# The normalised token rows keep their feature order, and the expert gather reads its stationary blocks with a step of eight elements

## The reference, cut to what matters

```
t = rmsnorm(x, norm_ffn)                       # (320, 1024)
combine = two experts of one group per token   # router
act = silu(t @ w_gate[e]) * (t @ w_up[e]) * combine
x = x + sum over e of act @ w_down[e]
```

## Time and profile before

| | |
|---|---|
| runs without the profiler | 1128.38 us median of 3 (1127.12 to 1129.35) |
| the profiled execution | 1124.03 us, its span 1122.3 us |
| PE busy, share of span | 947.8 us, 84% |
| DVE, ACT busy | 645.9 us (58%), 447.1 us (40%) |
| mean granted clock of PE | 0.921 |
| DMA | 203.33 MB, mean 181 GB/s |

### The profile page before, as it was taken

The page is one execution under the profiler, slowest core; times in us unless marked ns, Lnnn a source line. Parts: engine busy times, 40 slices in busy tenths (PEclk is TensorE's granted clock), DMA queues, the critical chain, the costliest instruction groups (busy, mean ns, idle before and its releaser), DMA issues.

```text
span 1122.3 us, 12426 instructions
## 1 busy us (share of the span) xinstructions
PE 947.8 (84%) x4149; PEld 688.6 (61%) x4149; DVE 645.9 (58%) x1206; ACT 447.1 (40%) x665; POOL 39.3 (4%) x75
## 2 busy tenths in 40 slices
PE   5899999999888687765699966989998999899685
PEld 3476776777554445432467755777777777677363
DVE  2329993001335545423647347788877787888574
ACT  0221102213122233122422044767766776677542
POOL 4000004000000000000000010000000000001100
PEclk9899999999859798897899976999999999999988
DMA  8042355332220676676303241877787788688501
GB/s 226 1 150 98 127 185 181 115 114 75 79 72 10 192 240 221 215 236 260 115 29 134 75 149 67 317 284 303 313 309 291 290 322 319 257 318 309 199 1 47
DMA packets 58069, 203.33 MB, mean 181 GB/s; under 512 B 8761, under 2 KB 9081, under 8 KB 51863
## 3 DMA queue, kind: packets, MB, share of 16 engines
q1 hardware_dynamic: 49280, 185.19, 45.5%
q10 hardware_dynamic: 6031, 9.19, 3.1%
q0 software_dynamic: 2704, 8.27, 2.3%
HBM read 188.96 MB, written 14.03 MB: 181 GB/s over the span
## 4 chain that ended last, share of the span: by engine, by line
PE 45%; DVE 9%; SPq 6%; issue 4%; ACT 4%; DMA 0%; DVEq 0%; POOL 0%; ACTq 0%
PE bank L1957 10%; PE bank L1959 10%; PE bank L1958 10%; PE bank L1948 5%; SPq L345 3%; SPq L348 3%; PE bank L2043 2%; PE bank L1879 2%; PE bank L2149 1%; PE bank L1844 1%; PE bank L2067 1%; DVE act_lo L1505 1%; PE bank L1797 1%; DVE h_tok L1360 1%; PE bank L1853 1%
## 5 line engine op out<-in xcount | busy, mean ns | idle before, releaser
L1669 PE MATMUL bank<-scratch,ring 128*128 128x320 f32 x896 | 242.5, 433 | 0.0
L1669 PEld LDWEIGHTS bank<-scratch,ring 128*128 128x128 f32 x896 | 169.8, 190 | 70.6 <-issue 0.5
L1454 DVE TENSOR_TENSOR pieces<-ring,pieces 128x1024 fp32r<-128x1024 f32 x144 | 173.3, 1222 | 43.3 <-ACT pieces L592 40.7
L592 ACT ACTIVATE pieces<-ring 128x1024 fp32r<-128x1024 f32 x144 | 150.8, 1060 | 76.7 <-PE bank L1959 70.2
L592 ACT ACTIVATE proj<-bank 128x512 f32<-128x512 f32 (+4 forms) x73 | 36.3, 506 | 157.5 <-PE bank L1669 117.0
L1081 DVE SCALAR_TENSOR_TENSOR proj<-scratch,par_w,proj 128x256 f32<-128x256 f32 x240 | 73.7, 380 | 1.1
L1957 PE MATMUL bank<-pieces,act_ft 128*128 128x512 f32 x96 | 43.0, 448 | 28.6 <-DVE act_lo L1505 28.6
L1454 DVE TENSOR_TENSOR last_piece<-ring,last_piece 128x1024 fp32r<-128x1024 f32 x48 | 58.6, 1221 | 2.3 <-ACT last_piece L592 0.3
L592 ACT ACTIVATE scratch<-bank 128x512 f32<-128x512 f32 (+5 forms) x42 | 20.5, 520 | 97.1 <-PE bank L1879 42.1
L592 ACT ACTIVATE last_piece<-ring 128x1024 fp32r<-128x1024 f32 x48 | 51.0, 1062 | 13.7 <-PE bank L1959 13.7
L1844 PE MATMUL bank<-ident,ring 128*128 128x128 f32 x256 | 38.3, 315 | 13.6 <-ACT proj L592 6.4
(11 more groups left out here) (384 smaller groups left out, 1665.1 us busy)
## 6 DMA issues: line engine op xcount, KB each, us to landing
ring<-in_w_expert_gate SPq DMA_DIRECT2D x16, 2048.0 KB, 7.9
ring<-in_w_expert_up SPq DMA_DIRECT2D x16, 2048.0 KB, 8.2
ring<-in_w_expert_down SPq DMA_DIRECT2D x16, 2048.0 KB, 7.8
ring<-in_w_in SPq DMA_DIRECT2D x14, 2048.0 KB, 7.8
ring<-in_cache_k SPq DMA_DIRECT2D x64, 256.0 KB, 3.2
ring<-in_cache_v SPq DMA_DIRECT2D x64, 256.0 KB, 3.1
moe_rows<-att ACTq DMA_DIRECT2D x16, 512.0 KB, 4.5
ring<-in_w_branch SPq DMA_DIRECT2D x3, 2048.0 KB, 9.9
```

The lines of the kernel that those rows point to most:

```text
L592: return F(out, in_, ACT.Copy)
L1454: TT(piece_of[r % 4][:, 1, :], raw_piece(EXPERTS + 3 * e, r), piece_of[r % 4][:, 0, :].bitcast(F32), ALU.subtract).then_inc(s("lo_ready"), 1)
L1669: m = MM(bank[t % 4][:, 0:T], slot(j, DC, GROUP)[:, k, (t % 4) * P:(t % 4 + 1) * P], h[:, k, :], start=k == 0, stop=k == DC - 1)
```

## The change

ACT's L838 and DVE's L1360 write `h_tok` in the order in which they read `x1`. The stationary block k is then every eighth element from k on, a step of 32 bytes; the view `h_of` names it, and the gather reads it. No instruction is added, removed or moved on any engine, and the moving operand, the PSUM banks and all waits are as they were. The last two pieces of the diff stand in a branch for crowded experts that these inputs do not take.

```diff
@@ (tiles)
         h_tok = in_place("h_tok", "gates", 0, [P, 5, D])
         PICK_OF = (0, 1, 0, 1, 2)
+        h_of = h_tok[:, :, :].rearrange("p i (m k) -> p i k m", k=DC)
@@ (ACT)
             def h_tok_hi(b):
                 act.wait_ge(s("rstd_ready"), 1 + b // 2)
-                F(by_parts(h_tok[:, (0, 1, 4)[b], :], DC), by_rows(x1[:, b, :], DC), ACT.Identity, scale=rstd[:, b:b + 1]
+                F(h_tok[:, (0, 1, 4)[b], :], x1[:, b, :], ACT.Identity, scale=rstd[:, b:b + 1]
                   ).then_inc(s("h_tok_hi_ready"), 1)
@@ (DVE)
-                STT(by_parts(h_tok[p, lo_, :], DC), by_rows(x1[p, b, :], DC), rstd[p, b:b + 1],
-                    by_parts(h_tok[p, hi_, :].bitcast(F32), DC), ALU.mult, ALU.subtract).then_inc(s("h_tok_ready"), 1)
+                STT(h_tok[p, lo_, :], x1[p, b, :], rstd[p, b:b + 1], h_tok[p, hi_, :].bitcast(F32), ALU.mult, ALU.subtract
+                    ).then_inc(s("h_tok_ready"), 1)
@@ (PE, gather)
                     for c in range(2):
-                        f = slice((2 * j + c) * P, (2 * j + c + 1) * P)
                         for i_ in range(5):
-                            m = MM(b_[:, c * 2 * P:(c + 1) * 2 * P], h_tok[:, i_, f],
+                            m = MM(b_[:, c * 2 * P:(c + 1) * 2 * P], h_of[:, i_, 2 * j + c, :],
                                    pick_t[:, PICK_OF[i_], :, :].rearrange("p u n -> p (u n)"), start=i_ == 0, stop=i_ == 4)
@@ (PE, the branch not taken)
-                        MM(bank[k % 4][:, t0:t0 + P], h_tok[:, i_, f].bitcast(F32), ident[:, :], start=i_ == 0, stop=i_ > 1,
+                        MM(bank[k % 4][:, t0:t0 + P], h_of[:, i_, k, :].bitcast(F32), ident[:, :], start=i_ == 0, stop=i_ > 1,
```

More of the change, by code:

```diff
@@ L2095, in _ @@
                         pe.wait_ge(s("h_hi_ready"), k - 3)
-                    f = slice(k * P, (k + 1) * P)
                     for i_, t0 in enumerate((0, P, 0, P)):
-                        MM(bank[k % 4][:, t0:t0 + P], h_tok[:, i_, f].bitcast(F32), ident[:, :], start=i_ == 0, stop=i_ > 1,
+                        MM(bank[k % 4][:, t0:t0 + P], h_of[:, i_, k, :].bitcast(F32), ident[:, :], start=i_ == 0, stop=i_ > 1,
                            skip_group_check=True)
-                    m = MM(bank[k % 4][:, SEQ:T], h_tok[:, 4, f].bitcast(F32), both_halves, start=False, stop=True,
+                    m = MM(bank[k % 4][:, SEQ:T], h_of[:, 4, k, :].bitcast(F32), both_halves, start=False, stop=True,
                            skip_group_check=True)
```

## The result

The changed kernel is slower: 1131.7 us against 1124.3 us for the kernel before, medians of 11 runs each, ratio 1.0052 with a 95% interval of 1.0031 to 1.0072. That is +5.9 us. The forecast was +5.3 us. The profiled execution of the changed kernel has a span of 1128.3 us, 6.0 more than the 1122.3 of before, so the two traces can be compared piece by piece.

The account below looks back on a forecast made before the run. PE was taken to bound the experts. Front -3.9, first groups +10.8, first expert +0.2, first forty +1.4, second groups 0 and clock -3.2 sum to +5.3 on 1128.4: 1133.7 us, range 1122.9 to 1151.

Parts of the forecast that it names:

- What bounds the kernel: Experts: PE sets the pace; first gather group on its path, +0.83 us in 13 turns; second hidden in a wait.
- The price of a load: Gather on PE: a stepped load takes 220 ns, adding 100 ns a matmul and 1.0 us a group of ten.
- Rival A: Gather loads on PE: a stepped load costs no more, only the front's gain remains, 1124.5 us; chance 0.22.
- rival B: Gather loads on PE: a stepped load costs three to four times, not twice; at 320 ns 1150.0 us; chance 0.13.
- B's dear end: Gather loads at the upper bound, 430 ns each, second groups also ending too late: +62.7 us, 1191.
- The first forty: First 40 gather matmuls, about 30 at clock 0.50: +0.4 us for these, +1.0 for the other ten, +1.4 in all.
- Rival C: Gather loads: the price counts in PE's own cycles, so the slow 30 matmuls double too; +11.2 us, 1139.6; chance 0.12.
- The front: Before the first gather: in-order row writes on ACT and DVE save 1.0 + 2.2 + 0.7, together -3.9 us.
- ACT's first write: Front: ACT's first h_tok write, on the path ahead of DVE's first, gets 1.0 us shorter.
- DVE's pair: Front: DVE's first two h_tok writes, 5.63 us together, get 2.2 us shorter, with POOL's work beside them.
- The third write: Front: DVE's third h_tok write, ahead of the ranking chain ending in pick_t, gets 0.7 us shorter.
- The clock: Gathering turns: PE's shorter wait brings four falls to 0.50 instead of six, 1.6 us each: -3.2 us.

Follow-up runs that it names:

- steps 2 and 4: Kernel before, permuted writes, every gather load reading elements 8 or 16 bytes apart; times not read, ten matmuls took 1.19 and 2.22 us.
- the kernel with early writes: Kernel before with ACT's root of the first two blocks and their row writes ahead of the copies turning the second block: 1118.3 us, ratio 0.9935.
- the second group alone: Kernel before, permuted writes, only the second gather group of each turn loading with the step of eight: 1118.5 us, ratio 0.9932.
- the nine matmuls: Kernel before plus nine unneeded 256-column matmuls on PE per turn, behind the second gather group: 1114.0 us, ratio 0.9912.
- the first group alone: Kernel before, permuted writes, only the first gather group of each turn loading with the step of eight: 1146.0 us, ratio 1.0172.
- step 32: Kernel before, permuted writes, gather loads reading elements 128 bytes apart from the first four planes; time not read, ten matmuls took 2.15 us.
- the loads alone: Kernel before with all gather loads at the step of eight and the writes still permuted: 1135.5 us, ratio 1.0080.
- the change on top of the move: Changed kernel with ACT's first two row writes also moved ahead of the second block's turning copies: 1128.5 us, ratio 1.0030 to the kernel before.
- writes alone: Changed kernel with the gather reading 128 adjacent elements again, so only the writes are in order: 1121.5 us, ratio 0.9963.

## Why the prediction was right

**What bounds the kernel.** Right. The first group of a turn is on PE's path (13 turns of +0.88 us, forecast 0.83), the second in the wait for `act_lo` (0.69 us left, forecast 0.9; a second group grew by 1.2 us, not 1.0).

**The price of a load.** A matmul of the gather went from 119 to 230 ns, +111 where I took +100, within the 92 to 123 of the bounds. A load of 230 ns is at most 1.8 ns a column, in the range of 1.7 to 1.9 ns that I had read from the other engines. But the hops in those rows are of writes as well (ACT's and L1499's of writes only), and the loads of PE are reads; that both have one cause was assumed, and no run tests it. The steps 2 and 4 show where the price begins and agree with a line of 16 bytes. Rival A is out by every trace with a step of 16 bytes or more, and rival B too. B's dear end, 2.4 ns a column, rested on DVE's 3.71 us, which belongs to POOL's company (below).

**The first forty.** +2.3 us where I had +1.4, the one term that is off by more than half. The step that was mis-sized is the load: I took 220 ns at either clock and found 9.77 us / 40 = 244 ns, about 0.12 us more a matmul than before at the full clock and 0.03 more at 0.50. (The 208 ns that I read at 0.50 before are a little low, since a count in a window takes in records that began ahead of it: by their starts those matmuls ran one in 213 ns.) Rival C expected 427 ns at 1.2 GHz. Its own test is the stretch at that clock:

```profile
682.00:686.00 4.00, 4.00 (x18) 4.00 (x18) 1.26 (x3) 1.79 (x3) 0.00 (x0) 0.50 0.00 0
687.00:691.00 4.00, 4.00 (x19) 4.00 (x18) 3.44 (x7) 3.21 (x6) 0.00 (x0) 0.95 0.00 0
```

The counts, 18 and 19 in 4 us, take in such records too, but they are alike. By the starts, a stepped matmul took 240 to 246 ns at 0.50 and 239 to 244 at the full clock: its load does not follow PE's clock. C is out.

**The front.** -3.46 us against -3.9. ACT's first write gave 0.97 and DVE's pair 3.15 (5.63 to 2.48), more than the 2.2 I took, since both ended before POOL's second instruction began. But POOL then met the next DVE instruction:

```profile
655.97 2.48 DVE L1353 SCALAR_TENSOR_TENSOR h_tok<-x,stat,h_tok 128x1024 fp32r<-128x1024 f32 x2 [1.22 <-ACT h_tok L831]
656.60 1.79 POOL L540 MEMSET scratch<- 16x2048 f32 x1 [290.45 <-PE bank L1952]
...
658.55 2.00 POOL L456 TENSOR_SCALAR_AFFINE_SELECT scratch<-scratch 16x2048 f32<-16x2048 f32 x1
659.08 2.02 DVE L1010 CUSTOM_DVE_ANT_0 rows<-x 128x512 f32<-128x512 f32 x1
```

L1010 takes 0.7 us elsewhere and 2.02 here. It is the select alone that costs. POOL's memset ran beside the in-order writes and they took their 1.28 us; in the kernel with early writes L1017 (L1010 here) took its 0.75 us beside that memset. Before the change the slow write, from 659.82 to 663.53, overlapped only the select, not both of POOL's instructions and ACT's second write as I had read it, and it lost 1.7 us; L1010 lost 1.3. So the sum came out near in part by luck: I had the loss on the second write, and it fell on L1010 (0.97 + 3.15 - 1.3 + 0.7 = 3.5). The third write gave its 0.7.

**The clock.** Three falls in the fourteen gathering turns in place of six and one behind them in place of none: -4.8 + 1.6 = -3.2 us, as forecast. The number was right and the reason was half of it. The wait that the second group fills takes falls away (six to one in the run with the second group alone, six to none with the nine matmuls). What I did not have is that the slow first group adds some (six to ten with the first group alone, its wait unchanged). That their sum came to my four was luck, for I had no way to work it out: the kernel with step 32 has six falls with nearly the same turns. The counts themselves come back: three in each of the three kernels with both groups stepped by eight (the change, the loads alone, the change on top of the move), six or seven in each of the four with fast loads and an open wait (before, writes alone, early writes, step 2). Each is the count of one execution, and executions of the kernel before range from 1119.6 to 1129.6 us with mean granted clocks of 0.930 to 0.915. What besides the wait decides a fall stays open.

## What to carry to other kernels

A layout has a cost on the side that writes and on the side that reads; count how often each runs and whether anybody waits for it. Here three writes each on two engines that could be idle stood against 320 loads on the engine that bounds the kernel, and it was better to keep the loads adjacent and move the writes. On PE, ask how far apart the elements of a stationary block lie: 8 bytes cost nothing here, 16 or more nearly doubled the time of a matmul.

When a matmul's load is about as long as its product, nothing hides a slower load, but a wait may. And where the bounding engine waits a little in each turn, read the granted clock after the wait: useless work in the gap gave 9.9 us here, though the wait alone did not tell how many falls a kernel had.

## What the runs showed of the hardware that I had not expected

- Under a matmul of 256 columns, a load of 128 fp32 columns on PE sets a pace of 213 to 252 ns a matmul from a step of 16 bytes on, nearly the same at either clock (241 and 243 ns in the first forty), and at 8 bytes no more than an adjacent one; a matmul with an adjacent load does follow the clock (119 against 213 ns).
- Slowing 140 loads made the kernel 7.7 us faster (ratio 0.9932), and adding 144 needless matmuls made it 9.9 us faster (0.9912), each time with turns as long as those without a fall before: what went were five and six falls of the granted clock to 0.50, 1.6 us each.
- DVE beside POOL: one 512-column instruction took 2.02 us in place of 0.7 while POOL ran a 16 x 2048 select, and a permuted row write 3.71 in place of 1.96; a memset of the same size beside DVE cost nothing.
